# Second scan: decays' differences and mask built in PSUM by TensorE, one exponential of 128x512 a head, skip term on GpSimd, chunks reordered

## The reference, cut to what matters

```python
seg = a_cum[:, :, :, None] - a_cum[:, :, None, :]           # per chunk: cum[l] - cum[s]
causal = jnp.tril(jnp.ones((CHUNK, CHUNK), dtype=bool))[None, None, :, :, None, None]
Lmat = jnp.exp(jnp.where(causal, seg, -jnp.inf))
cb = jnp.einsum('bclgn,bcsgn->bclsg', Cc, Bc)
y_diag = jnp.einsum('bclsg,bclsgr,bcsgrp->bclgrp', cb, Lmat, xdt)
decay_states = jnp.exp(a_cum[:, :, -1:] - a_cum)
states = jnp.einsum('bclgn,bclgr,bclgrp->bcgrpn', Bc, decay_states, xdt)
# h <- exp(a_cum[last]) * h + states, chunk after chunk; prev = the h before each chunk
y_off = jnp.einsum('bclgn,bcgrpn,bclgr->bclgrp', Cc, prev, jnp.exp(a_cum))
y = y_diag + y_off + d_skip * xh                             # the skip term
```

## Time and profile before

| what | us |
|---|---|
| device time, median of 3 runs (2946.67 to 2952.40) | 2949.12 |
| profiled execution, first to last instruction (span) | 2942.1 |
| median of the runs less that span (start and end of an execution) | 7.0 |
| stage of `ssd_prepare`, 2244.5 to 2286.1 | 41.6 |
| stage of `ssd_chunks`, 2286.1 to 2327.4 | 41.3 |

### The profile page before, as it was taken

One profiled execution on the slowest core, in us unless ns is written; L12 is line 12 of the kernel. 1 busy time (PEld: TensorE's weight loads), 2 busy tenths in 40 slices (PEclk: granted clock), 3 DMA queues, 4 the chain that ended last, 5 costly groups with the idle time before them and its releaser, 6 DMA issues. The chain is left out here.

```text
span 2942.1 us, 32467 instructions
## 1 busy us (share of the span) xinstructions
PE 2610.6 (89%) x11428; PEld 1791.2 (61%) x11428; DVE 1856.5 (63%) x3798; ACT 1293.4 (44%) x2876; POOL 681.1 (23%) x638
## 2 busy tenths in 40 slices
PE   6998987978888777799999999799898888999998
PEld 6886783434444222355555555598786556788887
DVE  6787467777777677777777776554655755433323
ACT  3244235444444444555566654444335355232222
POOL 3210003434444444444444434000000200000000
PEclk9999999999999999999999999999997799999999
DMA  6853048999999999999999999555230102123231
GB/s 245 291 168 119 23 165 323 415 410 420 420 420 406 420 408 418 417 409 419 419 414 409 420 405 414 194 182 178 81 93 18 38 23 86 65 86 97 91 106 72
DMA packets 131731, 750.81 MB, mean 255 GB/s; under 512 B 17408, under 2 KB 17936, under 8 KB 65248
## 3 DMA queue, kind: packets, MB, share of 16 engines
q0 software_dynamic: 81824, 575.43, 48.2%
q1 hardware_dynamic: 49744, 173.30, 17.0%
HBM read 746.57 MB, written 2.10 MB: 254 GB/s over the span
## 5 line engine op out<-in xcount | busy, mean ns | idle before, releaser
L1848 PE MATMUL peer_y<-rows,diag 128*128 128x512 f32 x2048 | 991.2, 610 | 171.5 <-ACT diag L1828 162.1
L1802 DVE CUSTOM_DVE_ANT_0 rows<-rows,hidden 128x1024 f32<-128x1024 f32 x512 | 627.9, 1226 | 358.2 <-DMA rows<-in_peer_table,experts 352.5
L1789 POOL DMA_INDIRECT rows<-in_peer_table,experts x512 | 599.7, 1171 | 978.2 <-PE peer_y L1848 764.1
L1848 PEld LDWEIGHTS peer_y<-rows,diag 128*128 128x128 f32 x2048 | 361.5, 191 | 583.2 <-ACT diag L1828 296.1
L1825 ACT ACTIVATE hid<-hid 128x1 f32<-128x1 f32 x512 | 103.1, 201 | 535.9 <-DVE hid L1802 531.9
L2451 DVE TENSOR_TENSOR piece_w_low<-piece_raw,piece_w_high 128x1024 fp32r<-128x1024 f32 x132 | 161.2, 1223 | 102.7 <-ACT piece_w_high L2446 102.6
L1828 ACT ACTIVATE diag<-ident,hid 128x128 f32<-128x128 f32 x512 | 206.4, 403 | 16.6
L2446 ACT ACTIVATE piece_w_high<-piece_raw 128x1024 fp32r<-128x1024 f32 x132 | 138.7, 1053 | 108.1 <-PE out_bank L152 77.5
L1826 ACT ACTIVATE hid<-hid,gates 128x1 f32<-128x1 f32 x512 | 151.8, 296 | 16.8
L150 PE MATMUL peer_y<-peer_feat_high,early_w_high 128*128 128x256 f32 x352 | 144.6, 411 | 2.2 <-issue 2.2
L426 ACT ACTIVATE proj_w_high<-proj_raw 128x1024 fp32r<-128x1024 f32 (+2 forms) x57 | 57.7, 1015 | 199.9 <-PE proj_pair L152 104.9
(11 more groups left out here) (569 smaller groups left out, 5554.7 us busy)
## 6 DMA issues: line engine op xcount, KB each, us to landing
ada<-in_w_ada POOLq DMA_DIRECT2D x96, 384.0 KB, 5.0
piece_raw<-in_ffn_w_gate SPq DMA_DIRECT2D x44, 512.0 KB, 3.5
piece_raw<-in_ffn_w_up SPq DMA_DIRECT2D x44, 512.0 KB, 4.4
piece_raw<-in_ffn_w_down SPq DMA_DIRECT2D x44, 512.0 KB, 3.5
query_raw<-in_peer_w_query SPq DMA_DIRECT2D x32, 512.0 KB, 7.0
early_raw<-in_ffn_w_gate SPq DMA_DIRECT2D x22, 512.0 KB
early_raw<-in_ffn_w_up SPq DMA_DIRECT2D x22, 512.0 KB, 14.4
early_raw<-in_ffn_w_down SPq DMA_DIRECT2D x22, 512.0 KB, 7.9
```

Source lines behind the costliest of these rows:

```text
L1789: pool.indirect_dma_start(self.rows[:, b, :], None, self.table, bass.IndirectOffsetOnAxis(ap=self.experts[:, unit % self.SETS, n % TOPK:n ...
L1802: dve.tensor_tensor_reduce(out=self.rows[:, b, 0:D], in0=self.rows[:, b, 0:D], in1=self.hidden[:, tile, :], scale=1.0, scalar=0.0, op0=ALU ...
L1848: last = pe.matmul(self.y[self.bank(tile)][:, c * BANK:(c + 1) * BANK], self.diag[:, b, :], self.rows[:, b, D + c * BANK:D + (c + 1) * BAN ...
```

## The change

In `second_projection` DVE zeroes a `[48, 512]` tile `cum_raw` and part of `y` at slab 0, and GpSimd's queue loads the mask, `d_skip` and two copies of `pick` (rows 0 to 15 and 32 to 47) into it. At slab 15 DVE makes `later`, an fp32r identity and the fp32r `pick` of 48 rows. Behind the running sum DVE makes its high part and its low remainder, and a transfer puts the remainder in rows 32 to 47.

In `ssd_prepare` a head's bank gets nine fp32r products: one of 512 columns (`pick` against the sums, high and low in one go), four of 128 columns that take cum[s] away, and four of 128 columns that add the mask. ACT takes one exponential of 128x512 from the bank. L2929, the bias and the load at the block's start are gone. Three row banks go round, freed by the exponential. The transposes start at head 2. GpSimd makes the skip term in eight products of 128x512.

In `ssd_chunks` the state of chunk 0 comes ahead of its diagonal, the state of chunk 1 right behind it, the skip term is gone from DVE, and `w_q_low` comes last. `state` and `carried` lie elsewhere in SBUF.

The diff, cut to its core:

```diff
@@ second_projection
+                pool.dma_start(mask, dram["causal_t"]).then_inc(m.consts, 16)
+                pool.dma_start(m.d_skip[:, :], dram["d_skip_2"].broadcast_to([P, SH])).then_inc(m.consts, 16)
+                pool.wait_ge(rows_clear, 2)
+                for at in (0, LOW_AT):
+                    pool.dma_start(pick_raw[at:at + SH, :, :], dram["pick"]).then_inc(m.consts, 16)
+                pool.wait_ge(low_ready, 1)
+                pool.dma_start(m.cum_raw[LOW_AT:LOW_AT + SH, :], soft[:, 3, :]).then_inc(m.cum_in, 16)
...
+            if n == CONSTS:
+                dve.wait_ge(m.consts, 64)
+                dve.tensor_scalar(m.later[:, :], mask, -1.0, float(2 ** 100), ALU.add, ALU.mult)
+                dve.tensor_copy(m.ident_r[:, :], t.ident[:, :])
+                link(dve.tensor_copy(m.pick[:, :, :], pick_raw[:, :, :]))
...
-                link(dve.tensor_tensor_scan(m.a_cum[:, :], keep[:, :], soft[:, 0, :], 0.0, ALU.mult, ALU.add))
+                link(dve.tensor_tensor_scan(m.a_cum, keep[:, :], soft[:, 0, :], 0.0, ALU.mult, ALU.add))
+                link(dve.tensor_copy(m.cum[0:SH, :], m.a_cum))
+                dve.tensor_tensor(soft[:, 3, :], m.a_cum, m.cum[0:SH, :].bitcast(F32), ALU.subtract).then_inc(low_ready, 1)
@@ ssd_prepare
-        @block.sync
-        def _(sp):
-            sp.dma_start(pick_in, dram["pick"].rearrange("k r p -> k (r p)")).then_inc(consts, 16)
...
             for r in range(SH):
-                if r >= 2:
-                    pe.wait_ge(masked, r - 1)
-                row = row_bank[r % 2][:, :, :].rearrange("p c s -> p (c s)")
-                pe.matmul(row, pick[:, r, :], cum.high[:, :], start=True, stop=False)
-                pe.matmul(row, pick[:, r, :], cum.low[:, :], start=False, stop=True).then_inc(rows_done, 1)
+                if r >= ROWS:
+                    pe.wait_ge(exps, r - ROWS + 1)
+                row = row_bank[r % ROWS]
+                pe.matmul(row[:, :, :].rearrange("p c s -> p (c s)"), m.pick[:, r, :], m.cum[:, :], start=True, stop=False)
+                for c in range(TT):
+                    pe.matmul(row[:, c, :], cum_neg[:, c * P:(c + 1) * P], m.pick[:, r, :], start=False, stop=False)
+                for c in range(TT):
+                    last = pe.matmul(row[:, c, :], m.ident_r[:, :], m.later[:, :], start=False, stop=(c == TT - 1))
+                last.then_inc(rows_done, 1)
                 if FIRST_TURN <= r < FIRST_TURN + XB + SG:
                     turn(pe, r - FIRST_TURN)
...
+            dve.wait_ge(m.cum_in, 16)
+            dve.tensor_scalar(cum_neg[:, :], m.cum_raw[:, :], -1.0, None, ALU.mult)
+            dve.tensor_copy(m.cum[:, :], m.cum_raw[:, :]).then_inc(neg_ready, 1)
...
             for r in range(SH):
-                if r + 1 < SH:
-                    hide_later(r + 1)
+                dve.wait_ge(exps, r + 1)
+                dve.tensor_tensor(m.between[:, r, :, :], m.between[:, r, :, :], m.cb[:, r // HPG, :, :], ALU.mult)
                 if FIRST_TURN + 1 <= r < FIRST_TURN + 1 + XB:
                     scaled(r - FIRST_TURN - 1)
-                dve.wait_ge(exps, r + 1)
-                dve.tensor_tensor(m.between[:, r, :, :], m.between[:, r, :, :], m.cb[:, r // HPG, :, :], ALU.mult)
...
+        @block.gpsimd
+        def _(pool):
+            pool.wait_ge(m.consts, 64)
+            for b in range(XB):
+                cols, heads = slice(b * P, (b + 1) * P), slice(2 * b, 2 * b + 2)
+                pool.wait_ge(moved_act, b + 1)
+                pool.tensor_tensor(by_head(m.y[:, :, cols]), by_head(m.x_tok[:, :, cols]),
+                                   m.d_skip[:, heads].unsqueeze(1).unsqueeze(3).broadcast_to([P, TT, 2, SHD]),
+                                   ALU.mult).then_inc(m.skipped, 1)
...
             for r in range(SH):
-                act.wait_ge(masked, r + 1)
-                for c in range(TT):
-                    last = act.activation(m.between[:, r, c, :], m.between[:, r, c, :], ACT.Exp, bias=neg_a[:, c, r:r + 1])
-                last.then_inc(exps, 1)
+                if r == SH - 1:
+                    act.wait_ge(squared, 2 * TT)
+                act.wait_ge(rows_done, r + 1)
+                act.activation(m.between[:, r, :, :], row_bank[r % ROWS][:, :, :], ACT.Exp).then_inc(exps, 1)
@@ ssd_chunks
+            states(0)
+            diagonal(0)
+            states(1)
+            diagonal(1)
+            for c in range(1, TT):
+                carry(c)
+                if 1 < c < TT - 1:
+                    states(c)
+                if c + 1 < TT:
+                    diagonal(c + 1)
```

More of the change, by code:

```diff
@@ L2816 @@
 LATENT_PARTS = ((0, QL), (QL, QL + KVL))
+LOW_AT = 32
+CUM_ROWS = LOW_AT + SH
 def ssd_prepare(core, t, dram, m):
     nc = core.nc
-    XB, FIRST_TURN = 8, 3
+    XB, FIRST_TURN, ROWS = 8, 2, 3
     with ExitStack() as ctx:
[L2825 to L2829, removed]
+        cum_neg, ones = m.cum_neg, m.between[0:SH, SH - 2, 0, :]
         sq = m.between[:, SH - 1, :, :].rearrange("p c s -> p (c s)")
         last_diag = sbuf(nc, ctx, "last_diag", [SH, TT, SH])
-        neg_a = sbuf(nc, ctx, "neg_a", [P, TT, SH])
         a_tok = sbuf(nc, ctx, "a_tok", [P, TT, 2, SH])
@@ L2973, in _, with ssd_chunks @@
                     move(act, r - FIRST_TURN)
[L2976 removed]
+def ssd_chunks(core, t, dram, m, a, room):
     nc = core.nc
@@ L2980, in ssd_chunks @@
     with ExitStack() as ctx:
-        state = sbuf(nc, ctx, "ssd_state", [P, 2, SG, G])
-        carried = sbuf(nc, ctx, "carried", [P, D])
+        state = room.sbuf("ssd_state", [P, 2, SG, G])
+        carried = room.sbuf("carried", [P, D])
         y_bank = [psum(nc, ctx, f"y_bank{i}", [P, D]) for i in range(2)]
@@ L2998, in _, with states, diagonal @@
         def _(pe):
-            for c in range(TT):
+            def states(c):
+                if c >= 1:
+                    pe.wait_ge(state_ready, c)
+                for g in range(SG):
+                    last = pe.matmul(s_bank[:, g * G:(g + 1) * G], m.b_tok[:, c, g, :], m.x_end[:, c, g * G:(g + 1) * G],
+                                     start=True, stop=True)
+                last.then_inc(state_done, 1)
+            def diagonal(c):
                 if c >= 2:
@@ L3005, in _, with carry @@
                 last.then_inc(diag_done, 1)
[L3006 to L3020 removed]
+            def carry(c):
+                pe.wait_ge(state_ready, c)
+                if c >= 2:
+                    pe.wait_ge(carry_used, c - 1)
+                for g in range(SG):
+                    last = pe.matmul(c_bank[:, g * G:(g + 1) * G], m.conv[:, 10 + g, c * P:(c + 1) * P],
+                                     state[:, c % 2, g, :], start=True, stop=True)
+                last.then_inc(carry_done, 1)
+            states(0)
[8 more added lines that the diff above has]
+                    diagonal(c + 1)
         @block.scalar
@@ L3390, in second_mixer_and_feed_forward @@
             a.w_q_split = core.sem("w_q_split")
-            ssd_chunks(core, t, dram, m, a)
+            ssd_chunks(core, t, dram, m, a, weights)
         a.out = Scratch(nc, LIMIT - 4 * TT * D, LIMIT).sbuf("mla_out", [P, TT, D])
```

181 lines of the change are left out of this document (90 added, 91 removed).

## The result

The changed kernel takes 2953.45 us (median of 20 runs, 2949.97 to 2959.66), the kernel before 2946.73 (20 runs on the same chip, 2940.28 to 2952.40): a ratio of 1.0023, 95% interval 1.0017 to 1.0029. It is 5 to 8.5 us slower; I had forecast 11 us faster. The profiled execution took 2957.04 us with a span of 2955.1, so only 1.9 us lie around a span. The two profiled executions differ by more than the medians do: 13.0 us in their spans, of which 9.2 had gone by when `ssd_prepare` began (2253.77 instead of 2244.57), 5.3 of them ahead of `second_projection`, where both kernels are the same. So I compare stage with stage.

A forecast was written before the change was run, and what follows sets the result against it. TensorE and DVE were taken to set the pace in turn in ssd_prepare, DVE in ssd_chunks. +1.1 - 4.9 - 7.6 = -11.4 us took the span from 2942.1 to 2930.7, forecast 2938 us, range 2926 to 2954.

The forecast's parts named there:

- The projection, +1.1: End of second_projection: DVE's added copy and subtraction of 16x512 lie on the path, +1.1 us, at most 1.4.
- The earlier start, 2.6 us: Start of ssd_prepare: load, wait and rounding of pick gone, so the first head starts at 2247.4 instead of 2250.05.
- A product of 128 columns, 0.11 full and 0.21 half: TensorE in the heads: price of a 128-column fp32r product in us, read from instructions of 64 columns.
- Now there is no such gap: TensorE in the heads: the gap from 2247.6, after which the clock fell, is gone; a head taken as 1.1 us.
- -4.9: ssd_prepare as a whole: ends at 2281.2 against 2286.1.
- the second of the signs of being wrong: Heads of ssd_prepare: a granted clock of 0.5 with TensorE never idle would show the forecast wrong.
- Rival (c): Heads: TensorE becomes the bound at the half clock, 3.3 us a head with transposes, stage +10, 2955; chance 0.18.
- GpSimd and DVE in turns: Heads: instructions with two SBUF inputs alternate, so eight GpSimd products of 1.2 us add 9.6 us to DVE's 20.2.
- the hold-up: Heads: DVE waiting for GpSimd's products; if GpSimd held nothing up, 18.4 us instead of 26.8, stage -13.
- The chunks, -7.6: ssd_chunks: 33.7 us against 41.3; 5 from the skip term, the rest from the earlier start.
- the bound for a late clock: ssd_chunks: a clock that rises only behind the second state, as late as now, brings -3.
- What lies around a span: Whole kernel: the median of the runs stands 7.0 us above the profiled span, so 2930.7 became a forecast of 2938.

The follow-up runs named there:

- x2_rows128: Changed kernel with pick, cum and cum_neg on 128 partitions instead of 48, the added rows zero: 2935.97 us, 0.9964 of the kernel before.
- x7: Changed kernel with 128 rows, skip term on DVE ahead of the first state, nothing on GpSimd: 2930.69 us, 0.9941 of the kernel before.
- x10: Changed kernel with 128 rows, skip term on DVE ahead of the first state, cb read from PSUM: 2928.89 us, 0.9939 of the kernel before.
- x1: Kernel before with only the new order of the chunks, skip term on DVE ahead of its wait: 2945.02 us, 0.9988 of the kernel before.
- x4: Changed kernel (48 rows) with the skip term on DVE ahead of the first state, nothing on GpSimd: 2954.07 us, 1.0020 of the kernel before.
- x11: As x10, with transposes of blocks 0 and 1 ahead of the heads, all others two heads earlier: 2931.51 us, 0.9941 of the kernel before.
- x6: Changed kernel with the chunks in the old order, skip term still from GpSimd: 2956.80 us, 1.0032 of the kernel before.

## Why the prediction was wrong

1. The projection, +1.1: right in size. DVE's timeline after shows the two added instructions, TensorE's the wait of the earlier trace rows, now 3.74 us instead of 2.72. No run tested it alone, but the wait is 3.73 to 3.75 us in all twelve profiles with this projection and 2.71 to 2.72 in the three without.

```profile
2237.10 0.41 DVE L2809 CAST cum_rows<-cum_raw 16x512 fp32r<-16x512 f32 x1
2237.55 0.68 DVE L2810 TENSOR_TENSOR soft<-cum_raw,cum_rows 16x512 f32<-16x512 f32 x1
```

```profile
2238.88 0.46 PE L150 MATMUL proj_bank<-proj_w_high,mix_feat_high 128*128 128x256 f32 x1 [3.74 <-DVE proj_w_low L432]
```

2. The earlier start, 2.6 us: right (2.55); from the stage's first instruction the first head starts after 2.95 us instead of 5.5.
3. A product of 128 columns, 0.11 full and 0.21 half: right (0.12 and 0.22).
4. **The step that failed is "Now there is no such gap", from which I had TensorE at the full clock in the heads.** TensorE had no gap, and the clock fell all the same. It made TensorE the bound and turned -4.9 into +11.0. This is the second of the signs of being wrong that I had named, a clock of 0.5 in the heads with TensorE never idle. x2_rows128 shows that the rows of the array in use make the difference: the same products with zero rows added, 1.00 instead of 0.50 and 34.8 us instead of 52.6. By x7 full rows are no guarantee. The Trainium skill ("TensorE: Matmul & The Clock Gate", Why this matters for your kernels) also asks for no idle gaps to stay warm; here 36.5 us without one were spent at the half clock, so the measurement decides against that as a sufficient rule. The row that could have warned me was the earlier trace rows: 0.50 for 30 us with TensorE busy 23 of them, while the projection ahead, with 128 rows, was at 1.00 from 2100 to 2210 us, where TensorE had no pause, and at 0.86 in the next 25 us, with 5 us of pauses. I laid it to one gap at the start. Rival (c) had the place and the size (3.3 us a head, +10, 2955), but I gave it 0.18, and for the wrong reason: I thought of short products and transposes, and x2 has them all at 1.00.
5. GpSimd and DVE in turns: the mechanism is right (1.41 instead of 0.69 us in seven of eight `x_end`), the size somewhat high: 6.0 us at the full clock for eight products, where I had 9.6. Hidden in the changed kernel.
6. With the clock up the forecast's stage is near what happens: it gives 36.7 us (2244.5 to 2281.2) against 34.8 in x2, with the hold-up sized too high. Without the hold-up it gives 28.3, and x10 took 28.3, which is partly luck, since x10 also drops the two copies of `cb`. The whole of x2 is 2936 against my 2938, or 10.6 us under the kernel before (0.36%) against my 11.4.
7. The chunks, -7.6: measured -7.45 in the profile. The size is right and the split is not. I had 5 us for the skip term and the rest for the earlier start; x1 and x4 show 3.5 for the new order with the skip term laid in a wait, 3.7 for a clock that rose some 5 us into the stage, as I had assumed (before, it rose at 2297.9, 12 us in; 2297.4 was misread from a row of 0.55), and at most 0.2 for taking the skip term off DVE. That the clock rose so early was luck in part: in x1, x10 and x11 it did not, and x1's -3.5 is near the -3 that I had as the bound for a late clock.
8. What lies around a span is 1.9 us, not 7.0: I had set one median against another execution's span. The forecast would have been 5 us lower for the profiled execution; for the median it did no harm.

With the terms as they were: +1.1 + 11.0 - 7.45 = +4.7, against 6.7 measured (5.0 to 8.5). The two other profiles of this stage with its four mask products at 48 rows (x4, x6) are 2.5 and 2.9 us longer, which would cover the rest; that the clock falls so early in most executions of the changed kernel is argued, not shown.

## What to carry to other kernels

Before counting on TensorE's full clock, look at the `K*M` of its products beside the granted clock: with 48 rows the clock fell although the engine never paused, and filling the operands to 128 partitions with zeros, which made no product longer (0.10 us instead of 0.12), took 0.59% off the changed kernel. It paid where TensorE worked without pauses; in the kernel before it brought nothing. Where GpSimd works beside DVE, let DVE take one operand from PSUM, and ask of a hold-up whether the held engine is the bound. Before a gain in a stage is put down to an edit, compare when the clock rose in both profiles: here that alone was worth 3.7 us in a stage whose instructions were the same.

## What the runs showed of the hardware that I had not expected

- Continuous work in which the sums' products had 48 rows: granted clock 0.50 for 36.5 us; the same with 128 rows: 1.00, in seven of eight profiles. The mask's products and the transposes had 128 rows in both.
- An fp32r product of 128 columns takes 0.12 us at the full clock with 48 rows and 0.10 with 128, and 0.22 at the half: about what a product of 64 columns takes.
- The exponential of 128x512 from PSUM takes 597 ns, as the copy of the same shape does (590).
- With the same instructions on TensorE, the clock fell some 2 us (x4, x6) or 5.7 us (the changed kernel) into `ssd_prepare`; the stage of 52.6 us is 2.5 to 3 us longer with the early fall. At 128 rows an early fall (x7) was followed by 20 us at 0.50.
- With the same instructions in `ssd_chunks`, the clock rose some 12.5 us (x1) or 5 us (x4) into the stage, 37.8 against 34.1 us.
